# Low halves of four token differences: from one group of four to four single steps inside the first seven-product chunk

## The reference

```
def swiglu(h, w_gu, w_down):
    gate, up = jnp.split(h @ w_gu, 2, axis=-1)
    return (jax.nn.silu(gate) * up) @ w_down
...
for li in range(DEPTH):                       # DEPTH = 2
    h = h + 0.5 * swiglu(rms_norm(h, ffn1_norm[li]), ffn1_w_gu[li], ffn1_w_down[li])
    u = rms_norm(h, mix_norm[li])
    ...                                       # layer 0: GLA, layer 1: HGRN2
    h = h + m
    h = h + 0.5 * swiglu(rms_norm(h, ffn2_norm[li]), ffn2_w_gu[li], ffn2_w_down[li])
    gate = jax.nn.sigmoid(rms_norm(h, ple_norm[li]) @ ple_w_gate[li])
    h = h + gate * (p[li] @ ple_w_proj[li])
return rms_norm(h, final_norm), ...
```

## Time and profile before

| | |
|---|---|
| median of three executions | 2256.8 us (2255.14 to 2256.95) |
| profiled execution | 2256.46 us, its span 2254.7 us |
| PE busy | 2238.1 us, 99% of the span |
| DVE, ACT, POOL busy | 1577.7, 1093.8, 395.6 us |
| DMA | 213.36 MB, 95 GB/s in the mean |

### The profile page before, as it was taken

The page is one execution under the profiler, slowest core; times in us unless marked ns, Lnnn a source line. Parts: engine busy times, 40 slices in busy tenths (PEclk is TensorE's granted clock), DMA queues, the critical chain, the costliest instruction groups (busy, mean ns, idle before and its releaser), DMA issues.

```text
span 2254.7 us, 41882 instructions
## 1 busy us (share of the span) xinstructions
PE 2238.1 (99%) x17570; PEld 2188.1 (97%) x17570; DVE 1577.7 (70%) x2136; ACT 1093.8 (49%) x1581; POOL 395.6 (18%) x271
## 2 busy tenths in 40 slices
PE   9999999999999999999999999999999999999998
PEld 9999999988899999999999999998999999999998
DVE  7888833657578888535788884359678688886344
ACT  7555523353545555423655562265465565555234
POOL 3222101112111221000222210005022212220001
PEclk9999999999999999999999999999999999999998
DMA  4333422324242333333233333322332333333231
GB/s 135 111 96 95 117 82 83 92 68 127 66 136 75 104 104 101 94 97 91 63 111 94 107 97 98 93 76 57 97 114 76 99 94 94 108 99 108 81 103 41
DMA packets 387338, 213.36 MB, mean 95 GB/s; under 512 B 7007, under 2 KB 381438, under 8 KB 387150
## 3 DMA queue, kind: packets, MB, share of 16 engines
q1 hardware_dynamic: 386928, 210.59, 32.9%
q10 hardware_dynamic: 190, 0.05, 0.0%
q0 software_dynamic: 32, 0.03, 0.0%
HBM read 198.98 MB, written 11.67 MB: 93 GB/s over the span
## 4 chain that ended last, share of the span: by engine, by line
PE 95%; ACT 2%; DVE 2%; issue 1%; DMA 0%; SPq 0%; POOL 0%; ACTq 0%; DVEq 0%
PE ps L564 46%; PE ps L635 37%; PE ps L769 5%; PE ps L807 2%; PE ps L867 1%; PE ps L927 1%; PE ps L942 1%; PE ps L898 1%; PE ps L848 1%; PE ps L783 0%; DMA w_raw<-in_ffn_w_gu_dram 0%; DVE w_low L1751 0%; PE ps L914 0%; PE ps L881 0%; PE ps L590 0%
## 5 line engine op out<-in xcount | busy, mean ns | idle before, releaser
L635 PE MATMUL ps<-u_diffs,w_high 128*128 128x272 f32 x2560 | 487.3, 287 | 2.2 <-DVE w_low L1751 1.7
L635 PEld LDWEIGHTS ps<-u_diffs,w_high 128*128 128x128 f32 x2560 | 401.6, 188 | 3.1 <-issue 3.0
L635 PE MATMUL ps<-u_diffs,w_low 128*128 128x272 f32 x1280 | 368.8, 288 | 0.0
L1655 DVE TENSOR_TENSOR w_low<-w_raw,w_high 128x1024 fp32r<-128x1024 f32 x205 | 262.8, 1299 | 92.3 <-ACT w_high L1111 92.0
L2334 POOL TENSOR_TENSOR hidden<-t_gate,t_up 128x544 f32<-128x544 f32 x84 | 191.5, 2280 | 714.9 <-ACT t_gate L1233 714.9
L564 PE MATMUL ps<-hid_high,w_high 128*128 128x272 f32 x1408 | 290.5, 287 | 0.0
L564 PE MATMUL ps<-hid_high,w_low 128*128 128x272 f32 x1408 | 289.5, 288 | 0.0
L564 PE MATMUL ps<-hid_low,w_high 128*128 128x272 f32 x1408 | 289.2, 287 | 0.0
L635 PE MATMUL ps<-u_high,w_low 128*128 128x272 f32 x960 | 278.3, 290 | 0.0
L635 PE MATMUL ps<-u_low,w_high 128*128 128x272 f32 x960 | 275.8, 287 | 0.0
L635 PE MATMUL ps<-u_high,w_high 128*128 128x272 f32 x960 | 275.3, 287 | 0.3 <-DVE w_low L1751 0.3
(11 more groups left out here) (280 smaller groups left out, 4218.9 us busy)
## 6 DMA issues: line engine op xcount, KB each, us to landing
w_raw<-in_ffn_w_gu_dram SPq DMA_DIRECT2D x176, 512.0 KB, 5.1
w_raw<-in_ffn_w_down_dram SPq DMA_DIRECT2D x64, 512.0 KB, 3.9
w_raw<-in_hgrn_w_in_dram SPq DMA_DIRECT2D x32, 512.0 KB, 4.1
w_raw<-in_gla_w_in_dram SPq DMA_DIRECT2D x25, 512.0 KB, 4.0
w_raw<-in_ffn_w_down_dram SPq DMA_DIRECT2D x32, 384.0 KB, 4.3
w_raw<-in_ple_w_gate_dram SPq DMA_DIRECT2D x16, 512.0 KB, 4.8
states_s<-in_state_gla_dram SPq DMA_DIRECT2D x8, 512.0 KB, 5.0
out_gla_s_dram<-states_s SPq DMA_DIRECT2D x8, 512.0 KB, 4.0
```

The costliest lines, as they stand in the source:

```text
L635: mm = pe.matmul(ps[:, bank, 0:HALF], half_slot(w, base, h)[:, k * P:(k + 1) * P], x(k), start=start and k == 0 and part == 0, stop=k == K ...
L1655: dve.tensor_tensor(WL[:, slot, :], RAW[:, slot, :], WH[:, slot, :].bitcast(F32), ALU.subtract)\
```

## The change

The helper that made the four low parts in one run is now a helper that makes one of them. DVE makes T2 where all four stood, T3 after `low_part(0, 1)`, T1 after `low_part(0, 2)` and T4 after `sum4(0)`. PE, which waited for all four ahead of product 4, now waits for one more of them ahead of each of the products 4, 2, 3 and 6. ACT, POOL and SP keep their instructions and order.

```diff
                 if k == 0:
-                    pe.wait_ge(s["diff_lo"], 4 * F + 4)
+                    pe.wait_ge(s["diff_lo"], 4 * F + 1)
                 pe.wait_ge(s["sum_lo"], nth(F, 5, k, 2))
                 pe.wait_ge(s["part_copied"], nth(F, 3, k, 1))
                 product(4, *diff(T2), b + 1, False)
                 product(1, block_of(UH, 1, 0), block_of(UL, 1, 0), b, False)
                 pe.wait_ge(s["sum_lo"], nth(F, 5, k, 3))
+                if k == 0:
+                    pe.wait_ge(s["diff_lo"], 4 * F + 2)
                 product(2, *diff(T3), b + 3, True)
                 pe.wait_ge(s["part_copied"], nth(F, 3, k, 2))
+                if k == 0:
+                    pe.wait_ge(s["diff_lo"], 4 * F + 3)
                 product(3, *diff(T1), b + 1, False)
                 pe.wait_ge(s["sum_lo"], nth(F, 5, k, 4))
+                if k == 0:
+                    pe.wait_ge(s["diff_lo"], 4 * F + 4)
                 product(6, *diff(T4), b + 2, False)
...
-            def diffs_low():
+            def diff_low(i, t, sign):
 
                 dve.wait_ge(s["diff_u"], 16 * F + 16)
-                for i, (t, sign) in enumerate(((T1, -1.0), (T2, -1.0), (T3, 1.0), (T4, -1.0))):
-                    dve.wait_ge(s["diff_hi"], 4 * F + i + 1)
-                    dve.scalar_tensor_tensor(out=TD[:, t, 1, :], in0=TDF[:, t, 1, :], scalar=sign,
-                                             in1=TD[:, t, 0, :].bitcast(F32), op0=ALU.mult, op1=ALU.subtract)\
-                       .then_inc(s["diff_lo"], 1)
+                dve.wait_ge(s["diff_hi"], 4 * F + i + 1)
+                dve.scalar_tensor_tensor(out=TD[:, t, 1, :], in0=TDF[:, t, 1, :], scalar=sign,
+                                         in1=TD[:, t, 0, :].bitcast(F32), op0=ALU.mult, op1=ALU.subtract)\
+                   .then_inc(s["diff_lo"], 1)
...
             if e:
                 gate_out(0)
-                diffs_low()
+                diff_low(1, T2, -1.0)
                 sums(0)
                 sum2(0)
                 low_part(0, 0)
             else:
                 sums(0)
                 sum2(0)
-                diffs_low()
+                diff_low(1, T2, -1.0)
                 gate_out(0)
                 low_part(0, 0)
             low_part(0, 1)
+            diff_low(2, T3, 1.0)
             gate_out(1)
             for k in range(NK):
                 if k:
                     out21(k - 1)
                 low_part(k, 2)
+                if k == 0:
+                    diff_low(0, T1, -1.0)
                 low_part(k, 3)
                 sum4(k)
+                if k == 0:
+                    diff_low(3, T4, -1.0)
                 if k:
                     out12(k - 1)
                 low_part(k, 4)
```

## The result

The changed kernel takes 2261.37 us (median of 22 executions, 2257.52 to 2263.92), the kernel before 2256.16 in the same series (22 executions, 2252.66 to 2258.83). The medians differ by 5.2 us; the ratio on record is 1.0021 with a 95% interval of 1.0015 to 1.0027, that is 3.4 to 6.1 us slower. The profiled execution took 2261.89 us, its span is 2259.9 us.

A forecast was written before the change was run, and what follows sets the result against it. PE, busy for 99% of the span, was taken as the bound, with DVE's lateness at chunk 1 deciding. FFN losses of 2.84, 0.89, 0.85 and 0.89, together 5.47 us, gave a median of 2262.3 us, range 2258.9 to 2264.2.

The forecast's parts named there:

- The bound: DVE's lateness at `low_part(1, 0)` when PE reaches chunk 1: no slack in FFN 0, 1.44 us in the others.
- The three added waits: PE's added waits in chunk 0 cost nothing; an uncovered one at most 0.15 us.
- The pauses ahead of chunk 1: PE waits about 1 us there in FFN 0, about 0.9 us in each other FFN, for `low_part(1, 0)`.
- The steps removed early: T1, T3, T4 leaving the place ahead of the gate evictions gain nothing, except 0.1 us allowed in FFN 2.
- The sum: Later DVE less slack at chunk 1, FFNs 0 to 3: 2.84, 0.89, 0.85, 0.89, together 5.47 us.
- The term for POOL's multiplication: It stretches a DVE step by 1.17 us: 0.69 more in FFNs 1 and 3, 1.03 in FFN 2, none in FFN 0.
- ACT's copy behind the high part of S4: In FFN 0 it delays product 3 by 2.4 us, to about 51.35, contained in the delay at chunk 1.
- The time: Whole kernel: predicted median 2262.3 us, 0.24% slower.
- Rival 1: Clock halves after PE's pause ahead of product 3 in FFN 0, up to 2.1 us more: 2263.4; chance 0.14.
- Rival 2: POOL's multiplication slips into a gap and FFNs 1 to 3 lose little: 2260.0, or 2258.9; chance 0.19.
- Rival 3: Product 4's wait in FFNs 1 to 3 is for DVE; early release saves up to 2.0 us: 2254.8; 0.07 with Rival 4.
- Rival 4: DVE is earlier at `gate_out(1)` than thought, so the change doesn't reach PE: 2256.8; chance 0.07 together with Rival 3.

The follow-up runs named there:

- the experiment without it: Changed kernel with POOL filling the second hidden block with zeros instead of multiplying, against the kernel before the change: 2256.43 against 2255.23 us, ratio 1.0003.
- FFN 0 alone: The change made only in FFN 0, FFNs 1 to 3 as before, against the kernel before: 2258.06 against 2256.16 us, ratio 1.0009.

## Why the prediction was right, point by point

- **The bound.** DVE's lateness at `low_part(1, 0)`, with no slack in FFN 0 and 1.44 us in the others, was the right place to look. The four waits of 0.56 us and less had nothing to do with the differences: none of them went. The three added waits cost nothing, as forecast: T4, the closest, ended at 51.91 in FFN 0, and product 6 starts twelve matmuls, about 1.5 us, behind product 3's 51.77. The pauses ahead of chunk 1 were forecast as about 1 us in FFN 0 and 0.9 in the others, and the timeline shows 0.62, 0.62, 0.33 and 0.61, since a pause is counted from the end of the last record; the shifts of the matmuls are what the sum foretold.
- **The steps removed early are worth nothing.** Right in FFNs 0, 1 and 3: DVE waits 3.51 us ahead of `gate_out(1)` in FFN 1. In FFN 2 they are worth 0.14 us, and there "PE waits nowhere for the low parts of the differences" was wrong by as much. In the kernel before, `low_part(0, 0)`, queued behind the four low parts, ended at 1121.98, and product 0 of chunk 0 started 0.15 us later (first two rows, DVE and PE): a pause too short for the list. In the changed kernel (last two rows) it ends at 1122.77, long before product 0:

```profile
1120.77 1.21 DVE L1751 TENSOR_TENSOR w_low<-w_raw,w_high 128x1024 fp32r<-128x1024 f32 x1
...
1122.13 0.36 PE L635 MATMUL ps<-u_high,w_high 128*128 128x272 f32 x1
...
1121.55 1.22 DVE L1756 TENSOR_TENSOR w_low<-w_raw,w_high 128x1024 fp32r<-128x1024 f32 x1
...
1127.50 0.29 PE L635 MATMUL ps<-u_high,w_high 128*128 128x272 f32 x1
```

- **The sum.** Forecast 2.84, 0.89, 0.85, 0.89 = 5.47; measured 2.74, 0.89, 0.73, 0.88 = 5.24. FFN 0 is 0.1 smaller: DVE's interval grew by 10.21 - 7.45 = 2.76, not 2.84. The three steps took their 3.60, but the idle time that they filled was 0.84 from start to start, not 0.76: `sum4` takes 0.60 (50.03 to 50.63), and before there were 1.44 from it to `low_part(0, 4)` (47.20 to 48.64). That FFNs 1 and 3 came out to 0.01 us is in part luck: the same 0.08 was too much there, and the first matmul behind a pause costs 0.07 that the sum does not have (704.38 to 704.58, where 0.13 is usual). In FFN 2 DVE came to `gate_out(1)` 0.2 us earlier (1127.76, less the 5.47 us by which the profile lies later there, against 1122.51 in the earlier trace rows), where I had allowed 0.1; that is the rest of its 0.85 against 0.73.
- **The term for POOL's multiplication.** Taken as 1.17 us from one row; the experiment without it gives 1.16. The figure worked out from the rule of the Trainium skill ("SBUF — State Buffer", section "Who interferes with whom"), the whole 1.36, would have made 0.2 us too much in each of FFNs 1 to 3; its statement that the two instructions shut each other out holds here (T1 took 2.45 us beside the multiplication, 1.28 without it), and the fill, which reads nothing, did not stretch T1.
- **ACT's copy behind the high part of S4.** Product 3 of FFN 0 was to start about 2.4 us later, at 51.35; it started at 51.77 in a profile that lies 0.44 us later there, which is 51.33, and 2.29 us of that show as a wait. The delay is contained in the later one at chunk 1, as the sum had it.
- **The time.** 2262.3 was forecast as a median from the three executions shown then (2256.8). Of the 0.9 us by which it is too high, 0.6 is that the longer series puts before at 2256.16, and 0.2 the sum.
- **Rival 1, the clock,** did not happen: 1.00 through FFN 0's pause in three profiles (the change twice, FFN 0 alone). It is a mechanism of this kernel all the same: at 3.50 us it did, for 0.6 us. The pause that the rival was built on does not bring the clock down every time: the pause of 2.60 us at the end of the kernel is in all nine profiles, and in seven of them the clock was still 1.00 when it ended (last section). So three profiles at 1.00 do not show that a pause of 2.29 us never brings it down.
- **Rival 2** fell: T1 (2.45 us) or `sum4` (1.86, 1.85, 1.86) is stretched in each FFN. **Rival 3** fell: the 0.56 us stayed, and it is ACT's copy. **Rival 4** fell with FFN 0's loss.

## What to carry to other kernels

A step that nobody waits for is not moved to its point of use for free: ask what the engine that runs it has next, and how much slack the consumer of that has. Here three steps stood where, but for FFN 2, their engine had to wait anyway, and were moved to where it had less idle time than they take. A wait for several semaphores is put down to the last of their updates, which can be one that the wait did not need, so count in the code what it waits for, and see whether the same wait, with the same length, has another name elsewhere, before building on it.

## What the runs showed of the hardware that I had not expected

The granted clock falls to 0.50 for a stretch in the mixers, among small matmuls and with PE busy, and not in the same place in each execution. In the changed kernel's profile it fell in the first mixer as well (stretches around 610 us), which cost the 1.5 us named above; in the profile of before the clock was 1.00 at that place and fell at 1602 (the first two rows are the changed kernel's, the third is of the kernel before):

```profile
606.00:610.00 4.00, 4.00 (x35) 3.84 (x35) 1.54 (x3) 1.26 (x3) 0.00 (x0) 1.00 0.00 0
611.00:613.50 2.50, 2.50 (x7) 1.47 (x7) 1.50 (x2) 1.92 (x5) 0.00 (x0) 0.50 0.00 0
...
1602.00:1604.50 2.50, 2.50 (x8) 1.47 (x7) 1.50 (x2) 1.96 (x4) 0.00 (x0) 0.50 0.00 0
```

In the repeat of the change it fell at 500 us and not near 1600. In all three profiles the fall came among 128x128 matmuls right behind groups of 32x32 and 128x32 ones (at 610.6 in a group that had started at 609.7, for one).

Of the 2.0 us that the changed kernel's profile won, 1.4 came at the end of the kernel, and they are the clock's as well. In the earlier trace rows it fell within the pause of 2.60 us, and the three matmuls behind it took 0.90 us; here it was still 1.00 behind the same pause, and they took 0.55 (PE, then a stretch):

```profile
2247.22 0.55 PE L1075 MATMUL ps<-ident,y_feat 128*128 128x128 f32 x3 [2.60 <-ACT y_feat L1128]
```
```profile
2247.20:2248.20 1.00, 0.98 (x10) 0.98 (x10) 0.00 (x0) 1.00 (x1) 0.00 (x0) 1.00 0.00 0
```

So the clock is most of what lies between the two profiles outside the FFNs, and it goes with the spread of one kernel's executions over 6 us: of the 22 of the changed kernel the four with a mean granted clock of 0.998 took 2257.5 to 2258.9 us, the four with 0.995 took 2261.6 to 2263.9. The eleven with 0.997 took 2258.8 to 2262.3, so that it explains the whole spread was not shown. For a change of a few us, matching the same instructions in two profiles told more than eleven timed executions.
